# Two-block sequence model on one core: where the q and k projections, the input maps, the turning tables and the attention gates' projections stand

## What is computed

```python
def second_block(x, ...):
    h = rms_norm(x, mix_norm_g[layer])
    u, q, k, v, f_logit, g_ssm, g_att = jnp.split(h @ w_in[layer], IN_SPLITS, axis=-1)
    y_ssm = s5_branch(u, ...)
    y_att = forgetting_attention(q, k, v, f_logit, ...)
    merged = jax.nn.sigmoid(g_ssm) * y_ssm + jax.nn.sigmoid(g_att) * y_att
    x = x + (merged @ w_out[layer]).astype(x.dtype)
    x = x + peer_ffn(rms_norm(x, ffn_norm_g[layer]), ...)

def s5_branch(u, ...):                       # 32 groups of 64 complex states
    lam = exp(a * step);  b' = coef * b      # b': the input map, scaled
    xr, xi = u @ b'.real, u @ b'.imag
    s[t] = lam * s[t-1] + x[t]               # complex, over 512 tokens
    y = s.real @ c_re - s.imag @ c_im
    z = gelu(y + d_skip * u) @ w_glu
    return val * sigmoid(gate)               # z split in two

def forgetting_attention(q, k, v, f_logit, ...):   # 8 heads of 128
    q, k = head_rms_norm(q, q_g), head_rms_norm(k, k_g)
    cum = cumsum(log_sigmoid(f_logit + f_bias))
    s = q @ k.T * scale + cum[q_pos] - cum[k_pos], causal
    return softmax(s) @ v
```

## Time and profile before

| | us |
|---|---|
| median of 3 runs | 3645.72 (3642.75 to 3648.36) |
| the profiled execution | 3641.11 |
| its span in the profile | 3639.4 |
| PE busy in it | 3375.2 (93%) |
| DVE busy | 2021.0 (56%) |
| ACT busy | 1057.9 (29%) |
| POOL busy | 488.4 (13%) |

### The profile page before, as it was taken

How to read it: one execution, slowest core, us unless ns; L and a number is a source line. 1 busy time by engine, 2 the same in 40 slices (tenths; PEclk the granted TensorE clock), 3 DMA queues, 4 the chain that set the end, 5 groups by cost and what they waited for, 6 DMA issues and landing times.

```text
span 3639.4 us, 37684 instructions
## 1 busy us (share of the span) xinstructions
PE 3375.2 (93%) x14636; PEld 2628.6 (72%) x14636; DVE 2021.0 (56%) x3634; ACT 1057.9 (29%) x1380; POOL 488.4 (13%) x216
## 2 busy tenths in 40 slices
PE   6999899989999555999798999999999999999999
PEld 6866678868787321776466888888888878888887
DVE  4556624257567899363434385856661055555554
ACT  2155332223232200242223323345553211111111
POOL 0000000004140023000000134432223300000000
PEclk6988899999999777999789999999999999999999
DMA  4133323322232001321012234448777465555553
GB/s 176 35 107 109 109 77 122 97 75 89 91 97 71 26 18 32 101 85 54 22 35 75 93 131 139 139 128 200 190 189 209 158 208 185 187 189 190 186 186 121
DMA packets 271922, 430.59 MB, mean 118 GB/s; under 512 B 146944, under 2 KB 147072, under 8 KB 271488
## 3 DMA queue, kind: packets, MB, share of 16 engines
q1 hardware_dynamic: 140544, 394.61, 32.7%
q10 hardware_dynamic: 131200, 33.55, 4.9%
HBM read 358.90 MB, written 69.21 MB: 118 GB/s over the span
## 4 chain that ended last, share of the span: by engine, by line
PE 84%; DVE 12%; ACT 2%; issue 1%; POOL 0%; DMA 0%; DVEq 0%; ACTq 0%; POOLq 0%
PE psum L493 84%; DVE st L1534 1%; DVE wl L1147 1%; DVE st L1542 1%; DVE st L1539 1%; PE psum L723 1%; DVE lb L1344 0%; ACT wh L815 0%; DVE bt L1513 0%; DVE bt L1514 0%; DVE n L1295 0%; DVE yb L1353 0%; DVE y L1348 0%; DVE probs L1623 0%; DVE sin L1242 0%
## 5 line engine op out<-in xcount | busy, mean ns | idle before, releaser
L1147 DVE TENSOR_TENSOR wl<-ring,wh 128x1024 fp32r<-128x1024 f32 (+2 forms) x320 | 373.9, 1171 | 994.8 <-ACT wh L815 994.5
L493 PE MATMUL psum<-h_hi,wh 128*128 128x512 f32 x2144 | 866.5, 404 | 53.5 <-DVE h_lo L1289 21.0
L493 PE MATMUL psum<-h_lo,wh 128*128 128x512 f32 x2144 | 850.5, 397 | 0.0
L493 PE MATMUL psum<-h_hi,wl 128*128 128x512 f32 x2144 | 850.2, 397 | 0.0
L815 ACT ACTIVATE wh<-ring 128x1024 fp32r<-128x1024 f32 (+2 forms) x492 | 504.1, 1027 | 945.8 <-PE psum L493 902.7
L1787 POOL TENSOR_TENSOR wl<-ring,wh 128x1024 fp32r<-128x1024 f32 x172 | 425.7, 2475 | 2114.7 <-ACT wh L815 2114.7
L493 PEld LDWEIGHTS psum<-h_hi,wh 128*128 128x128 f32 x2144 | 405.1, 189 | 157.9 <-issue 40.9
L493 PEld LDWEIGHTS psum<-h_hi,wl 128*128 128x128 f32 x2144 | 405.2, 189 | 100.1
L493 PEld LDWEIGHTS psum<-h_lo,wh 128*128 128x128 f32 x2144 | 405.7, 189 | 92.8 <-issue 3.3
L493 PE MATMUL psum<-ews_hi,wh 128*128 128x512 f32 x1024 | 408.7, 399 | 0.7 <-ACT ga L1117 0.7
L493 PE MATMUL psum<-ews_hi,wl 128*128 128x512 f32 x1024 | 403.5, 394 | 0.0
(11 more groups left out here) (357 smaller groups left out, 4062.4 us busy)
## 6 DMA issues: line engine op xcount, KB each, us to landing
ring<-tables SPq DMA_DIRECT2D x256, 512.0 KB, 3.6
acts_scratch<-ga SPq DMA_DIRECT2D x128, 256.0 KB, 2.1
gates_scratch<-stage ACTq DMA_DIRECT2D x8, 4096.0 KB, 27.1
abuf<-acts_scratch SPq DMA_DIRECT2D x128, 256.0 KB, 3.8
gbuf<-gates_scratch SPq DMA_DIRECT2D x128, 256.0 KB, 4.1
ring<-w_up SPq DMA_DIRECT2D x44, 512.0 KB, 3.5
ring<-w_modb SPq DMA_DIRECT2D x32, 512.0 KB, 3.6
ring<-w_moda SPq DMA_DIRECT2D x16, 512.0 KB, 3.6
```

What stands on the lines that cost most here:

```text
L493: return nc.tensor.matmul(out, lhsT, rhs, start=first, stop=last, **kw)
L1147: TT(wl, slot(t, 0, size[t]), wh.bitcast(F32), ALU.subtract).then_inc(S("low_by_ve"), 1)
```

## The change

1. **Input maps.** The 16 maps are made in the merging stage of block one: map 2n behind gr, map 2n+1 behind gg. PE transposes, ACT copies and issues a transfer to DRAM (`states_scratch`). Each has a ring tile of its own (256 columns, not split).
2. **Tables.** Built in 4 batches of 4 chunks, two beside down0 and two beside down1, each parked in the same DRAM tensor by a transfer on ACT's queue.
3. **State-space loop.** SP loads cos, sin and map of a chunk (`statew`) and its c (`outw`), three buffers deep. A q or k projection stands in each of the 16 chunks, with its head sum and norm. POOL's two differences are gone: DVE writes four turned parts, and PE makes four products.
4. **After the loop** gs and glu in another order (four gs first), then f, then v.
5. **Attention** as a pipeline: ga n, transposes of head n, scores of head n+1, product of head n; two sets of four PSUM banks.

```diff
+BESIDE = [f"q{n}" for n in range(HEADS)] + [f"k{n}" for n in range(HEADS)]
+AFTER = ["gs0", "gs1", "gs2", "gs3", "glu0", "gs4", "glu1", "gs5", "glu2", "gs6", "glu3", "gs7", "glu4", "glu5", "glu6",
+         "glu7"]
+IN_HEADS = [f"ga{n}" for n in range(KD)]
...
+            def state(c):
+
+                for k in range(2):
+                    sp.wait_ge(S(f"bt_parked{k}"), 16 * (NS // 2))
+                sp.wait_ge(S(f"tables_parked{c // 4 % 2}"), 16 * (c // 8 + 1))
+                if c >= 3:
+                    sp.wait_ge(S("out_done"), c - 2)
+                sp.dma_start(statew[:, c % 3, :], states_d[c]).then_inc(S(f"state_loaded{c % 3}"), 16)
+                sp.dma_start(outw[:, c % 3, :], io["w_ssm"][c][:, 2 * P:4 * P]).then_inc(S(f"state_loaded{c % 3}"), 16)
...
             for n in range(KD):
                 project(f"gr{n}", h)
+                input_map(2 * n)
                 project(f"pr{n}", yr, ready="yr_ready" if n == 0 else None, parts=(5, 5))
                 project(f"gg{n}", h)
+                input_map(2 * n + 1)
                 project(f"pg{n}", ygs, ready="yg_ready" if n == 0 else None)
...
             def states_out(c):
-                pe.wait_ge(S("s_ready"), 2 * (c + 1))
                 if c % 4 == 0:
                     wait(pe, S("ys_read"), c // 4)
-                t = TILE[f"ssm{c}"]
-                mm(psum[:, 7, :], wchunk(t, 2), ssm_s[:, 2 * (c % 2), :], c % 4 == 0, False)
-                mm(psum[:, 7, :], wchunk(t, 3), ssm_s[:, 2 * (c % 2) + 1, :], False, c % 4 == 3).then_inc(PE, 1)
+                for k, part in enumerate((0, 2, 1, 3)):
+                    pe.wait_ge(S("turned"), 4 * c + k + 1)
+                    last = mm(psum[:, 7, :], outw[:, c % 3, part // 2 * P:(part // 2 + 1) * P], turned[:, part, :],
+                              c % 4 == 0 and k == 0, c % 4 == 3 and k == 3)
+                last.then_inc(S("out_done"), 1)
...
             states_in(0)
             for c in range(NS):
+                if c:
+                    states_out(c - 1)
+                if c:
+                    head_sum(c - 1)
+                project(BESIDE[c], h)
                 if c + 1 < NS:
                     states_in(c + 1)
-                tile_here(pe, TILE[f"ssm{c}"])
-                states_out(c)
...
             for hd in range(HEADS):
...
+                project(IN_HEADS[hd], h, high=True)
                 pe.wait_ge(S("p_ready"), NB * (hd + 1))
...
+                if hd + 1 < HEADS:
+                    scores(hd + 1)
...
-            turns = [(0, 0, 12), (1, 0, 12), (2, 0, 12)], [(3, 0, 12), (4, 0, 12)], [(5, 0, 12), (6, 0, 12)], \
-                [(7, 0, 6)], [(7, 6, 12)], [(8, 0, 4)], [(8, 4, 8)], [(8, 8, 12)]
+            turns = [(0, 0, 4), (1, 0, 4), (2, 0, 4), (3, 0, 4)], [(4, 0, 4), (5, 0, 4), (6, 0, 4)], [(7, 0, 4)], \
+                [(8, 0, 2), (8, 2, 4)]
...
+                TT(turned[:, 0, :], st[:, 1, :], cc, ALU.mult).then_inc(S("turned"), 1)
+                STT(turned[:, 2, :], st[:, 1, :], -1.0, ss, ALU.mult, ALU.mult).then_inc(S("turned"), 1)
                 ve.wait_ge(step, 4 * c + 4)
...
+                STT(turned[:, 1, :], st[:, 3, :], -1.0, ss, ALU.mult, ALU.mult).then_inc(S("turned"), 1)
+                STT(turned[:, 3, :], st[:, 3, :], -1.0, cc, ALU.mult, ALU.mult).then_inc(S("turned"), 1)
+                if c >= 2:
+                    head_norm(c - 2)
```

More of the change, by code:

```diff
@@ L285, in build @@
         fcv = psum[:, 6:8, :]
[L286 to L296, removed]
-        gl = ar("gl", B + 21504, 6)
-        qT, kT, vt2 = ar("qT", B + 6144, HEADS), ar("kT", B + 10240, HEADS), ar("vt2", B + 14336, NB, D)
-        ht = ar("ht", B + 18432, 6)
-        fl = [ar(f"fl{k}", B + (k * T if k < 4 else 21504 + (k - 4) * T), 1)[0:HEADS, 0, :] for k in range(8)]
@@ new lines, in build @@
+        bt1, bt2 = (ar(f"bt{k}", B + 26624 + P * k, 1, P)[:, 0, :] for k in range(2))
+        u2, st = ar("u2", B, KS), ar("st", B + 2048, 4)
+        qT, kT = ar("qT", B + 4096, HEADS), ar("kT", B + 8192, HEADS)
+        ysh, ysl = both("ys", B + 12288, KS)
+        mg2, turned = ar("mg2", B + 16384, KD), ar("turned", B + 17408, 4)
+        outw, statew = ar("outw", B + 19456, 3, 2 * P), ar("statew", B + 20480, 3, SW)
+        ysk, ht = ar("ysk", B + 24320, 1)[:, 0, :], ar("ht", B + 24832, 4)
@@ L500, in three, with project @@
                 return mm(out, wl, xh[:, c, :], False, last)
-            def project(name, act, ready=None, at=0, parts=(KD,)):
-                b, k, kc = BLOCK[name], 0, sum(parts)
-                block_free(pe, b)
+            def project(name, act, ready=None, at=0, parts=(KD,), high=False):
+                k, kc = 0, sum(parts)
+                if high:
+                    upper_free(pe, HIGH[name])
+                    out = upper(HIGH[name])
+                else:
+                    block_free(pe, BLOCK[name])
+                    out = bank(BLOCK[name])
                 for i, chunks in enumerate(parts):
@@ L511, in project @@
                             pe.wait_ge(S(ready), at + k + 1)
-                        last = three(bank(b), whl(e, kk), act, k, k == 0, k == kc - 1)
+                        last = three(out, whl(e, kk), act, k, k == 0, k == kc - 1)
                         k += 1
@@ new lines, in _ @@
+            for hd in range(HEADS):
+                name = IN_HEADS[hd]
+                to_gate(name, True)
+                if hd:
+                    act.wait_ge(S("merged2"), hd)
+                    A(mg2s[0][:, hd - 1, :], mg2[:, hd - 1, :], ACT.Copy).then_inc(S("mg2_high"), 1)
+                if hd + 1 < HEADS:
+                    exponentials(hd + 1)
+                b = HIGH[f"mixed{hd}"]
+                upper_here(act, b)
+                A(qT[:, hd, :], upper(b), ACT.Copy).then_inc(S("o_ready"), 1)
@@ L1437, in _ @@
                 v.memset(ffp[k], 0.0).then_inc(S("ffpads_zero"), 1)
+            for k in range(2):
+                ve.wait_ge(S(f"bt_parked{k}"), 16 * (NS // 2))
             norm(1, 2, a2, mod[:, 24:32, :])
@@ L1480, in _ @@
                     half = int(name[4])
-                    if half:
-                        for k, lo, hi in turns[n]:
-                            angles(tables[0], k, lo, hi)
+                    if half and n % 4 == 0:
+                        ve.wait_ge(S(f"tables_parked{n // 4}"), 16)
+                    for k, lo, hi in turns[n % 4]:
+                        angles(2 * half + n // 4, k, lo, hi)
+                    if n % 4 == 3:
+                        ve.sem_inc(S("table_ready"), 1)
                     add_to_x(f"down{half}_", n, "x_ffn", mod_t[:, 2 * n + 80:2 * n + 81])
```

510 lines of the change are left out of this document (284 added, 226 removed).

## The result

The changed kernel takes 3517.24 us (median of 4 runs, 3516.8 to 3518.42) against 3644.23 us for the kernel before (4 runs): a ratio of 0.9652, 95% interval 0.9635 to 0.9669. The forecast was 3514 us in a range of 3490 to 3552, so time, sign and range held. The sum was not as good as that: two of its five terms were off by more than 4 us, one by 5 and one, which had its sign wrong, by 8 the other way, so that they cancel for the most part.

What follows compares the result with a forecast made beforehand. The loop was taken as bound by DVE, q and k by PE, so they were overlapped. Terms -23 + 4 + 97 + 16 + 35 = 129 us off 3641.1 gave 3512, median 3514 us, range 3490 to 3552.

Steps and rivals of the forecast that it cites:

- Part 3: State-space loop laid together with the q and k projections: 301 us against 398.4, a gain of 97 us.
- cost 53 us of the loop: In the loop: head norms, free beside a full PE before, were now to cost 53 us.
- Rival A: Loop clock stays at 0.76 because of PE's gaps, making PE the bound: 3540 to 3550 us, chance 0.15.
- E: Rival: DVE slowed by transfer traffic in the loop, 1 us a chunk, 3530 us, chance 0.04.
- Part 1: Input maps in the merging stage, where PE is full: 23 us lost, bounds 19 to 28.
- the first map does not [lie beside]: Merging stage: the first map stands behind DVE's chunks of yg, so pr0 starts 11.7 us late.
- Part 2: Tables built beside down0 and down1: net 4 us gained, bounds -6 to +8, with 5 us less for down1.
- I find 1 to 2 us of wait: Beside down0: DVE ends some 12 us late, but PE's halves made ahead leave only 1 to 2 us of wait.
- Part 4: Forget gate put ahead of v, its gap filled by v: 81.1 us becomes 65, 16 us gained.
- Part 5: Attention with ga as a pipeline: a head costs 17.3 us, eight 138 against 172.5, 35 us gained.
- rival C: Pipelines fail to overlap: attention heads wait 2.75 us or more again, down0 loses its lower bound; 3546 us, chance 0.10.
- Product and ga cover the 2.75: Attention: product and ga (8 us) between scores and transposes cover each head's 2.75 us wait for the shares.

## Why the prediction was right, point by point

**What bounds the kernel.** Right. The loop was DVE's before and after, 210.25 of 213.9 us, and the two runs with a cheaper norm show it. The chunk came out as summed from the earlier trace rows, 13.43 us from turn to turn:

```profile
1310.13 2.48 DVE L1674 TENSOR_TENSOR st<-psum,statew 128x512 f32<-128x512 f32 x4 [0.83 <-PE psum L566]
...
1319.51 3.35 DVE L1665 RECIPROCAL ht<-ht 128x512 f32<-128x512 f32 x1
1322.89 0.75 DVE L1666 SCALAR_TENSOR_TENSOR qT<-qT,small,ht 128x512 f32<-128x512 f32 x1
1323.56 2.47 DVE L1674 TENSOR_TENSOR st<-psum,statew 128x512 f32<-128x512 f32 x4
```

**Part 3, 97 forecast, 94.4 measured.** To the last turned part 208.6 us against 207, PE's chunk 11.60 as summed; the other 1.5 us of the shortfall lie ahead of the loop and behind it. Mis-sized was the skip: it held PE 6.3 to 7.2 us, not 4.7, since DVE comes to it behind a head norm; the run with the skip first shows that this costs nothing while DVE is the bound. That the norms "cost 53 us of the loop" is true of DVE's sum alone; taken out, they free 29.6, since PE's 11.60 then rule. Rival A failed though its mechanism exists. Timeline of PE behind a skip, then the clock of the stretches 1349 to 1355 and 1357 to 1363:

```profile
1351.19 5.83 PE L566 MATMUL psum<-turned,outw 128*128 128x512 f32 x8 [6.29 <-DVE ysk L1652]
```

```profile
1349.00:1355.00 6.00, 3.81 (x5) 1.75 (x6) 5.96 (x9) 0.00 (x0) 0.00 (x0) 0.50 0.00 0
...
1357.00:1363.00 6.00, 6.00 (x26) 4.53 (x25) 6.00 (x6) 2.60 (x3) 0.00 (x0) 1.00 0.64 218
```

Behind a wait of 6.29 us the clock was at its lower level, 1.2 GHz, for the four out products (5.83 us), and at 2.4 GHz again with the projection. E had nothing in it: beside 88 GB/s the low half of DVE took 1.21 and 1.22 us, as in the earlier trace rows, which is how the Trainium skill (SBUF — State Buffer, "SBUF: two separate sides") has it.

**Part 1, -23 forecast, -18.0 measured**, a little outside the bounds of 19 to 28. The wait was as said (11.4), the clock 1.6 and not 2.5, and the failed term is that of the transposes: 16 x 0.55 was taken from rows at half clock, and the run with the low halves moved shows 0.33 at full clock. The step "the first map does not [lie beside]" named a real wait, but was wrong in that it made the map its only cause: the run with the map first shows a low half waiting in the same queue.

**Part 2, +4 forecast, -4.1 measured.** Down1 gained 4.1 (5 forecast). The step that failed is "I find 1 to 2 us of wait" beside down0. The waits for `wl` were 4.9 us, and the clock of 0.97 from 974 to 1040 adds about 2 (3% of 61 us). DVE began its last addition of down0 at 1048.60, so that the next convolution came late as well; but that cost PE no wait, for PE is full at a clock of 1.00 from 1040 to 1155. The sum had 69 us of DVE against 61.5 of PE and counted no operation at more than its duration alone, though POOL's low halves run there. That was a row to be looked for, and the earlier trace rows had one: `bt` of the same size takes 1.28 us in the loop, with POOL at work, and 0.28 ahead of it, where POOL is idle. Beside down1 the 10.24 us charged to DVE for a product hold 1.9 us in which it waited for a high half; the 5 us of gain there were right all the same. Moving the tables away gives the price of the place, 6.8 us.

**Part 4, +16 forecast, +17.5 measured**, and undoing it costs 20. The sum had only PE's idle time; the clock behind the gap was missing from it.

**Part 5, +35 forecast, +37.9 measured.** The head is 15.6 us and not 17.3, again since the transposes and the product of the earlier trace rows were taken at a lower clock (0.50 over the transposes, 0.84 over the product). One head of the changed kernel on PE:

```profile
1703.02 1.25 PE L812 MATMUL psum<-ident,probs 128*128 128x128 f32 x10
1704.11 0.39 PE L566 MATMUL psum<-kT,qT 128*128 128x128 f32 x2
...
1710.87 2.32 PE L566 MATMUL psum<-probsT,vt 128*128 128x512 f32 x8
1712.95 0.48 PE L566 MATMUL psum<-h_hi,wh 128*128 128x512 f32 x1
```

The ten transposes take 1.09 us from start to start, not 2.19, the product 2.08, not 2.58. Closing the gaps raised the clock, and so the work itself became cheaper: a term that the sum did not have. The number owes something to luck. Eight heads were priced 13.5 us too dear, and the sum took them for the whole stage, which is 9.7 us longer than eight times 15.6: a wait for `probsT` came once, 3.9 us in the last head, by the mechanism of rival C, and the rest is clock, 0.88 up to the first transposes, 0.90 in the second head and 0.50 in the last product. "Product and ga cover the 2.75" was too generous to ga: the product covers 2.15 of it.

**The sum.** It gave 3512 us for the profiled execution, which took 3518.42 (span 3516.2). The median, taken as 4.6 us above that execution since it stood so before, is 1.2 us below it. These two errors of 6 us cancel, and so the median came out closer than the sum was: that is luck. Where the clock of a stretch falls once more or less is worth as much.

## What to carry to other kernels

When work of two engines is laid together, sum a period for each: the longer one is the new time, and what is taken from it later helps only down to the other (here 13.43 down to 11.60 us). Before you put a wait down to one operation, look at what stands behind it in the same queue, since the next one may be due at nearly the same moment. Price matmuls by rows at the clock that the stage will have after the change, and price DVE's operations on two SBUF inputs apart where POOL is at work.

## What the hardware showed that I had not expected

- An operation of DVE on two SBUF operands of 256 or 512 columns took 2.66 to 2.81 us instead of 0.42 to 0.69 beside an operation of POOL of 2.4 to 2.7 us, and one of 128 columns on a single large SBUF operand 1.3 instead of 0.28 beside one of 2.2 or 1.3 us.
- A transposition of 128x128 costs 0.11 us at full clock and 0.22 at half (ten in 1.09 and 2.19 us), so these small operations follow the granted clock as the large ones do.
- A reciprocal of 128x512 costs DVE 3.35 us, five times a product; the logarithm and exponential that took its place and that of the root cost ACT 1.3 us and two loads of 1.283 us.
- Behind single gaps of 4.6, 6.3 and 11.4 us PE lost only 2.6, 2.2 and 1.6 us to slow steps, and a loop with gaps of up to 12.9 us kept a mean clock of 0.90.
- The clock also fell where PE had no wait: behind the first scores of the changed kernel it was 0.61 from 1663 to 1667, and 0.79 from 1689 to 1697, with PE busy throughout. In the run with the skip first it stayed at 1.00 over the same heads.
